# Moving the weight splits behind other work in two places of a six-layer model kernel

## The reference

```python
def rmsnorm(x, g):
    y = x * rsqrt(mean(x * x, axis=-1) + 1e-6)
    return y * g

def fox_mixer(h, w_in, b_f, q_gain, k_gain, w_out):      # 16 heads of 64
    q, k, v, gate, f = split(h @ w_in)                    # 4 x 1024 and 16 columns
    q = rmsnorm(q per head, q_gain) * 64 ** -0.5
    k = rmsnorm(k per head, k_gain)
    c = cumsum(log_sigmoid(f + b_f))                      # over the tokens
    s = q @ k.T + (c[query] - c[key]), masked causally    # per head
    o = softmax(s) @ v
    return (o * sigmoid(gate)) @ w_out
```

## Time and profile before

| | |
|---|---|
| median of 3 runs | 2431.13 (2427.98 to 2431.22) |
| the profiled execution | 2425.49, its span 2423.9 |
| busy share of the span | PE 94%, PEld 89%, DVE 64%, ACT 50%, POOL 25% |
| granted TensorE clock, mean | 0.976 |
| ring_lo on VectorE | 740.8 in 372 instructions |
| ring_hi on ScalarE | 611.8 in 372 instructions |

### The profile page before, as it was taken

One profiled execution on the slowest core, in us unless ns is written; L12 is line 12 of the kernel. 1 busy time (PEld: TensorE's weight loads), 2 busy tenths in 40 slices (PEclk: granted clock), 3 DMA queues, 4 the chain that ended last, 5 costly groups with the idle time before them and its releaser, 6 DMA issues.

```text
span 2423.9 us, 48151 instructions
## 1 busy us (share of the span) xinstructions
PE 2268.8 (94%) x19050; PEld 2157.7 (89%) x19050; DVE 1555.5 (64%) x2520; ACT 1207.1 (50%) x1861; POOL 611.7 (25%) x738
## 2 busy tenths in 40 slices
PE   4999999999999899989998999998999999899998
PEld 4878999899999778789997889997798998788998
DVE  4665654746554675466556665657767976767994
ACT  4555444544544642355445555544556654456653
POOL 3113211013211020031111132115234534123540
PEclk9999999999999999999999999999999999999999
DMA  4324545424546312135453235555353555343554
GB/s 168 104 89 139 174 157 181 150 87 135 177 153 196 100 59 67 43 137 173 159 189 96 97 117 181 183 176 186 105 188 131 181 169 175 97 137 132 183 167 137
DMA packets 52863, 344.03 MB, mean 142 GB/s; under 512 B 5904, under 2 KB 7120, under 8 KB 20176
## 3 DMA queue, kind: packets, MB, share of 16 engines
q1 hardware_dynamic: 51984, 336.26, 42.0%
q0 software_dynamic: 704, 5.31, 0.5%
HBM read 340.43 MB, written 1.05 MB: 141 GB/s over the span
## 4 chain that ended last, share of the span: by engine, by line
PE 72%; DVE 11%; ACT 8%; issue 5%; DMA 1%; POOL 1%; DVEq 0%; ACTq 0%; SPq 0%
PE ps L763 70%; ACT ring_hi L1492 3%; DVE ring_lo L2027 3%; ACT arena L1492 3%; ACT hrs L1492 1%; DVE newt L2044 1%; DVE hrs L2045 1%; DVE newt L2043 1%; DVE arena L2136 1%; PE ps L952 1%; ACT sq L1492 1%; POOL arena L2903 0%; DMA ring<-in 0%; ACT L1492 0%; DMA ring<-out 0%
## 5 line engine op out<-in xcount | busy, mean ns | idle before, releaser
L763 PE MATMUL ps<-arena_r,ring_hi 128*128 128x272 f32 (+1 forms) x6688 | 1592.1, 287 | 13.1 <-DVE arena L2164 5.4
L763 PEld LDWEIGHTS ps<-arena_r,ring_hi 128*128 128x128 f32 x6688 | 1167.7, 191 | 21.1 <-issue 7.3
L763 PE MATMUL ps<-y_r,ring_hi 128*128 128x272 f32 (+1 forms) x3424 | 1014.1, 296 | 38.0 <-DVE ring_lo L2027 23.7
L2027 DVE TENSOR_TENSOR ring_lo<-ring,ring_hi 128x2048 fp32r<-128x2048 f32 (+2 forms) x372 | 740.8, 1992 | 387.8 <-ACT ring_hi L1492 385.9
L763 PE MATMUL ps<-y_r,ring_lo 128*128 128x272 f32 (+1 forms) x3424 | 982.9, 287 | 0.0
L763 PEld LDWEIGHTS ps<-y_r,ring_hi 128*128 128x128 f32 x3424 | 655.4, 191 | 62.2 <-issue 37.7
L1492 ACT ACTIVATE ring_hi<-ring 128x2048 fp32r<-128x2048 f32 (+2 forms) x372 | 611.8, 1647 | 117.5 <-DMA ring<-dn 48.6
L763 PEld LDWEIGHTS ps<-y_r,ring_lo 128*128 128x128 f32 x3424 | 657.4, 192 | 0.0
L763 PE MATMUL ps<-arena_r,ring_lo 128*128 128x256 f32 (+1 forms) x1632 | 465.2, 285 | 0.0
L763 PEld LDWEIGHTS ps<-arena_r,ring_lo 128*128 128x128 f32 x1632 | 309.4, 190 | 0.0
L1492 ACT ACTIVATE arena<-arena 128x272 f32<-128x272 f32 (+7 forms) x200 | 93.2, 469 | 381.1 <-DVE arena L2597 262.6
(11 more groups left out here) (234 smaller groups left out, 1711.5 us busy)
## 6 DMA issues: line engine op xcount, KB each, us to landing
ring<-gu SPq DMA_DIRECT2D x88, 1024.0 KB, 5.1
ring<-dn SPq DMA_DIRECT2D x64, 704.0 KB, 4.0
ring<-up SPq DMA_DIRECT2D x44, 1024.0 KB, 5.1
ring<-fox_in SPq DMA_DIRECT2D x32, 1024.0 KB, 5.1
ring<-sdn SPq DMA_DIRECT2D x32, 704.0 KB, 4.1
ring<-gdn_in SPq DMA_DIRECT2D x16, 1024.0 KB, 5.1
ring<-in SPq DMA_DIRECT2D x16, 1024.0 KB, 5.1
ring<-gla_in SPq DMA_DIRECT2D x12, 1024.0 KB, 5.1
```

The lines of the kernel that those rows point to most:

```text
L763: return nc.tensor.matmul(dst, w, mv, start=start, stop=stop)
L2027: V.tensor_tensor(ring_lo[:, slot, cols], ring[:, slot, cols], ring_hi[:, slot, cols].bitcast(F32), ALU.subtract).then_inc(lo_ready, 2 if ...
```

## The change

Nothing is computed differently; only the place of the splits changes. In the first norm, the two splits of the first block go, on ScalarE, from ahead of chunks 0 and 1 to ahead of chunks 2 and 4; on VectorE, from behind all sums to ahead of the sums of chunks 2 and 4. In both FOX stages ScalarE's hook `before(t)` goes behind the log-sigmoid (t = 1) and the square of a q or k tile, and still stands ahead of the exponentials. VectorE's hook `after(t)` goes from ahead of the evacuation to behind the evacuation, the forget logits (t = 0) and the row minima.

```diff
@@ ScalarE, norm_x
                 for c in range(KC):
-                    if base is None and c < 2:
-                        before(0, c)
+                    if base is None and c in (2, 4):
+                        before(0, c // 2 - 1)
@@ ScalarE, fox
-                    before(t)
                     if t == 1:
                         log_sigmoid()
                     if part in "qk":
                         act.wait_ge(evacuated, BANKS + n.tile + t + 1)
                         i = n.head + 2 * c + (part == "k")
                         fn(sq[:, i % 2, 0:T], raw[:, (2 * c + (part == "k")) % 3, :], ACT.Square).then_inc(hsq_ready, 1)
+                    before(t)
                     for u in in_slot(units, t):
                         exponent(u)
@@ VectorE, fox
-                    after(t)
                     evacuate(t, part, c)
                     if t == 0:
                         forget_logits()
                     for u in in_slot(units, t):
                         largest(u)
+                    after(t)
@@ VectorE, the first norm
             for c in range(KC):
+                if c in (2, 4):
+                    split(0, c // 2 - 1)
                 if c == KC - 1:
                     low_of_last(x, "norm_mix0", T)
                 sum_squares(c, T)
             n.norm += 1
             v.wait_ge(tables_loaded, 32)
-            split(0, 0)
-            split(0, 1)
             narrow_low(0, 1)
```

## The result

| | before | after |
|---|---|---|
| median of 5 runs | 2431.22 (2427.98 to 2437.72) | 2418.12 (2415.86 to 2427.04) |
| the profiled execution | 2425.49, span 2423.9 | 2416.58, span 2415.0 |
| granted TensorE clock, mean | 0.976 | 0.973 |

The ratio of the times is 0.9938 (95% interval 0.9918 to 0.9958): 0.6% faster, 10 to 20 us. The forecast was 2417.8 with a range of 2409 to 2426.

The account below looks back on a forecast made before the run. TensorE was taken as the bound, so moves pay only where it stands still. 6.2 + 2.0 - 1.9 + 2.7 + 2.85 + 1.45 = 13.3 off a median taken as 2431.1 gave 2417.8, range 2409 to 2426.

Parts of the forecast that it names:

- The start: Start of the program, first norm: last low part on GpSimd ends at 22.75 instead of 28.93, a gain of 6.2.
- The prediction's other sum: Whole kernel: if the narrow product behind tile 0 runs at 1.2 GHz, total gain 12.3 instead of 13.3.
- The log-sigmoid: Each FOX stage: tile 0 evacuated once rstd is there, so the log-sigmoid starts 1.0 earlier; 2.0 together.
- starts at 35.75: First FOX stage, old times: log-sigmoid follows ScalarE's high split at 35.75 instead of 36.78.
- Tile 4: Each FOX stage: low split behind the first minima delays q3's head norm, a loss of 0.95; 1.9 together.
- Tiles 10, 16, 22: k tiles with a split, both FOX stages: splits stay in series, 0.45 of 2.1 won at each; 2.7 together.
- Rival 1: FOX stages: only the start pays, k-tile stalls stay; 7.6 of gain, 2423.5; chance 0.2.
- q and v tiles: Tiles 6, 12, 18 and 8, 14, 20 of the FOX stages: TensorE doesn't wait there, taken as 0.
- The ends: End of each FOX product: last evacuation comes earlier, by 2.85 in the first stage and 1.45 in the second.
- The clock: Whole kernel: shorter stalls should have no more clock dips; 0 in the sum, up to 6 more gain.
- Rival 2: Whole kernel: shorter stalls have fewer clock dips, 6 more; gain 19, time 2412; chance 0.15.
- Rivals 3 and 4: 3: moved low split stalls all fourteen even tiles per stage, 2442.5, chance 0.04; 4: start gives nothing, 2424, chance 0.06.

## Why the prediction was right, step by step

The total was right (13.3 forecast; 13.1 between the medians, with an interval from 10 to 20; 8.9 between the profiled executions). That it fits to 0.2 is luck: of the terms, the start came 1.8 short and the second log-sigmoid 0.7 or more, the loss at tile 4 didn't come as described, and the clock, which had 0, took up to 2.9 at one place and gave about 1.5 at others. By stage, the sum had 10.45 up to the end of the first FOX product (6.2, 1.0, -0.95, 1.35 and 2.85), measured 9.9; and 2.85 in the second, measured 3.8. What the profiled executions lack beyond that went in the unedited stages, together with the clock; no run settles more about it.

- **The start, 6.2: mechanism right, size 4.4.** The splits and the later chunks came within 0.8 of where they were put; the table load and with it chunks 0 and 1 came earlier, which won nothing, since the high split waits for its data. The last chunk comes to TensorE 5.6 earlier (23.42, 28.98 before); GpSimd took 0.6 more than forecast, and the half rate took 1.1, as the kernel with 18 idle matmuls shows. The prediction's other sum, with 1 for the half rate, was 12.3, and the size of that 1 was right. It follows a rule of the Trainium skill (TensorE: Matmul & The Clock Gate, Part 1), and the trace of after agrees with it: the first matmuls are 0.22 apart and those from 27.9 on 0.125. I should have taken this term, since the first matmuls of before are at 0.43 each as well.
- **The log-sigmoid, 1.0 twice: right once.** In the kernel after it starts 5.5 earlier (7.2 forecast), 4.4 of it from the start and 1.1 from the hooks. In the second stage the lead grows from 6.3 to 6.6 only, and with the hooks alone the first log-sigmoid gains 0.17. The step that failed is "starts at 35.75": it counted ScalarE's queue and not the bias, which VectorE can't finish beside GpSimd's MEMSET. Shown by the kernel with the fills held back. In the first stage of after the 1.0 came by luck: the start's edit had moved the fills out of the way, the bias ends at 31.01, and the high split lets the log-sigmoid go at 31.30.
- **Tile 4, a loss of 0.95 twice: mechanism shown elsewhere, absent in after.** VectorE's hook alone has the wait in the first stage (0.84 against 0.20), both hooks alone in the second (0.85). In the kernel after TensorE ran tile 5 at half clock (granted 0.50 from 48.5 to 55.3) and came too late to wait. So "the wait up from 0.2 to 1.1" was wrong as a sign: the wait is 0. That the lead still fell by 1.2 there in the first stage, near the 0.95, is luck; it was lost to the clock and not to the norm, and in the second stage 2.5 were.
- **Tiles 10, 16, 22, 0.45 each: right.** The gap went from 2.52 to 2.02 at tile 10, from 2.57 to 2.03 at tile 16, from 2.52 to 2.39 only at tile 22, and from 2.71 to 2.18 or 2.19 three times in the second stage: 2.75 together, 2.7 forecast. That the rest stays because the splits are in series was shown in two ways. Rival 1 (only the start pays) is refuted: the hooks alone give 0.9949.
- **q and v tiles, 0 each: right.** No new wait for the head norm, `hrs` or the scaled rows is in the lists above.
- **The ends, 2.85 and 1.45: mechanism right, sizes 2.2 and 0.9.** In the first stage the lead grows from 6.2 to 8.4 at the last evacuation (204.20, and 195.80 after), where the wait for the meta rows (0.9) went and that for the evacuation fell from 3.7 to 2.5 (near 2.0 forecast). It then grows to 9.9, since before has a stretch at half clock behind this wait (204.65 to 208.05) and after has none: luck again. In the second the wait fell from 1.7 to 0.8.
- **The clock, 0.** Rival 2's 6 more didn't come: the mean granted clock is 0.973 and was 0.976. The dips lie at other places and are longer in sum, by about 14. Place by place the 0 was wrong: a dip of before that went gave about 1.5 (tile 10), and one that came took as much (tile 16).
- **Rivals 3 and 4:** no split on the path at other even tiles, and the start did give 4.4 in the trace. In the times its 3.2 has an interval from 0 to 6.3, and beside VectorE's hook the start adds nothing that can be told, so that it gives something rests on the traces. Among the chances one doesn't add up: rival 3 has 0.04, and "slower" only 0.03.

What I could have read and didn't: with the high split of the earlier trace rows left at 85.82, the low one would start at 87.8 in either order, but behind the evacuation and the minima it runs beside the exponentials and the root, and all 2.1 of the stall goes, 12.8 in six. The prediction had this figure as a bound, but only for a low split behind the head norm, which it excluded. VectorE's hook alone showed it with the low split still ahead of that norm, and that ScalarE's part of the change gives most of it away.

## What to carry to other kernels

A work item with a half on each of two engines is two moves: ask of each alone which one is on the path. Here the low half wanted to go behind the evacuation and the high half wanted to stay early, and moving both left the wait at 1.6 to 2.0 of 2.1 to 2.3. Before a chain is counted on to come earlier, list what the other engines run in the stretch that it moves into; a fill that nobody waits for held it for up to 2.7.

## What the runs showed of the hardware

- VectorE's TENSOR_SCALAR from SBUF to SBUF (16x272, 0.35 alone) didn't end while GpSimd ran a MEMSET of 2x4352 (3.73). It ended 0.15 behind the end of the second MEMSET in all 17 stages, of the 24 in the twelve traces, in which it began 0.35 or more before that end, and took from 0.51 to 3.06 by how early it began. VectorE's TENSOR_TENSOR with two inputs in SBUF isn't stopped by it (the split at 34.28 took 2.27 in it). The Trainium skill, SBUF — State Buffer, Who interferes with whom, has a rule for both: a `tensor_scalar` of VectorE in a two-port mode and GpSimd exclude each other for a whole instruction, and an operation with two SBUF inputs contends only with a GpSimd instruction that reads. The trace agrees. That this `tensor_scalar` runs in such a mode no row states; it takes 0.35 alone where the TENSOR_TENSOR of the same size ahead of it takes 0.43. Read beforehand the rule would have spoken against the 1.0 of the log-sigmoid.
- The other side of it: a GpSimd TENSOR_SCALAR that takes 0.49 took 2.19 and 2.86 beside a 2.29 low split of VectorE. That was in the forecast from the earlier trace rows; the kernel with the later split shows that it moves with the split.
- ScalarE's table load ran at 0.73 to 2.01, ahead of the wait for the inputs and not behind it (forecast 6.9 to 8.15). At the start of before it stood behind its first wait (9.37). The traces show the two places and not what decides between them.
- At the start of the program matmuls followed at 0.22 while the records have a granted clock of 1.00 there (13.7 to 16.2 and 18.9 to 27.9). The start-to-start time of the matmuls shows the rate in that stretch; the column doesn't.
